# Thirty-two experts on one core: pairs sorted by load, some cut into four parts of 32 rows, gathers issued one scatter earlier

## The chip, the cores and the metric

The kernel runs on 1 core of one Trainium2 chip. Its time is in device microseconds (us), from one execution of the whole program; the median of several executions stands for a kernel. The engines are PE (TensorE, matrix products), DVE (VectorE), ACT (ScalarE), POOL (GpSimd) and SP (SyncE), which here only issues DMAs. "PEld" rows are PE's loads of the stationary operand. TensorE's clock has two levels, 1.2 and 2.4 GHz; the profile shows the granted share (1.00 or 0.50).

## The reference

The program is two transformer blocks over 512 tokens of width 1024. The change lies in the last stage, a mixture of 32 experts with two experts chosen for each token:

```python
hf = h.reshape(-1, d_)                                   # 512 x 1024
g_logits = hf @ w_rg + b_rg                              # 4 groups; the best one is taken
e_sel = take(e_logits.reshape(-1, 4, 8), g_idx)          # its 8 experts; the best two are taken
weights = pg_top * pe_top / sum(pe_top)                  # 512 x 2
for e in range(N_EXPERTS):                               # 32
    act = silu(hf @ w_gate[e]) * (hf @ w_up[e])          # 1024 -> 256
    y = y + combine[:, e:e+1] * (act @ w_down[e])        # 256 -> 1024
```

There are 1024 choices (512 tokens, two each). Counting them with the reference on its inputs gives these loads, for experts 0 to 15: 39, 70, 43, 25, 39, 44, 50, 74, 35, 40, 48, 23, 34, 23, 28, 19, and for experts 16 to 31: 32, 18, 11, 17, 13, 16, 15, 18, 16, 27, 16, 44, 45, 47, 14, 41.

## The kernel before

Everything up to the expert stage is a long run of split matrix products (`pieces`) fed by slabs of weights from SP. It is not changed. The rows of the second normalisation are written to DRAM (`h2_dram`), unsorted, and the residual to the output (`out_columns`).

The expert stage works in **tiles** of 128 rows. Tile `t` carries two experts, 64 rows (`CAP`) for each: one from 0 to 15, one from 16 to 31. An expert with more than 64 rows overflows; its further rows are packed in blocks of 64. Tile 3 (`OVER`) holds the first two such blocks and loads the weights of their experts again. So there are 17 tiles (`BASE`), and behind an `If` (`more_tiles`) up to 13 more with one block each, which are entered where over two blocks are needed. With the loads above two experts (70 and 74 rows) overflow by one block each, so 17 tiles run.

For each tile, in this order:

- POOL `gather(t)`: an indirect DMA brings the tile's rows of `h2_dram` to `Xg`, by the row numbers in `tok` (or `tok2`, which come later). Two buffers.
- PE `transpose_rows(t)` (L3058); ACT and DVE copy the result, scaled, to `XT` (`xt_copy`, L1516, L2452).
- PE `gate_up(t)` (L3080): eight steps over the width, in each one product of 512 columns for each half, its output in PSUM partitions 0 to 63 or 64 to 127, so in one or the other half of the array's columns. A float32 product shows as two records, so a tile has 32.
- ACT `silu`, DVE `gated` (L2457), PE `transpose_act` (L3066), ACT `act_copy`, PE `down(t)` (L3097): 16 records.
- DVE `y_scaled(t)` (L2465) to `Yt`, then POOL `scatter(t)` (L977): an indirect DMA that adds the rows to the output. A scatter waits for the one before it to have landed. The tile `OVER` needs two, one for each half (`tokover`), since a token can stand in both.

PE puts `transpose_rows(t + 1)` between `gate_up(t)` and `transpose_act(t)`. SP loads the weights of expert `e` in three DMAs of 1 MiB, gate and up into one of 7 slots, down into one of 6. A gate/up slot is used again when the tile seven expert places back has finished `gate_up` (`gu_done`), a down slot when the tile three back has finished `down` (`y_done`). The experts of tiles 0 to 2 are fixed, and most of their weights are loaded before the stage. SP loads tile 3 when the overflow experts are known (`overflow_ready`) and the residual is stored (`out_set`), and then the rest in the order of the experts.

The row numbers come from a chain on DVE: ranks within an expert, `tok` (`tokens_ready`), the places of the overflow rows (`rows_with`, `pairs_with`), then for the overflow tile `tok2` (`over_tokens`) and the gate weights by row (`wtab`). Rank within an expert to row of the tile is a match against the constant vector `iota` by a product on PE (L3028, L3035).

Of the kernel before, what the change touches and what calls it, by code (L numbers as in the profile page):

```python
# [25 lines left out]
P = 128  # L26
# [27 lines left out]
BASE = NE // 2 + 1  # L54
NPAIR = BASE + NOV - 2

OVER = 3
# [264 lines left out]
def shared_events():  # L322
# [19 lines left out]
    for chain, events in CHAINS.items():  # L342
        n = 0
        for event, count in events:
# [15 lines left out]
               ("base_ready", 1), ("tokens_ready", 1), ("spots_ready", 1), ("overflow_ready", 1), ("over_tokens", 1),  # L360
               ("choice_weights", 1)],
# [10 lines left out]
def build_program(nc, a, out):  # L372

    ctx = ExitStack()
    with ctx:
# [155 lines left out]
        inpair = [at("inpair0", T0 + 3.75, [2 * NB, 2, NPAIR], BF16), at("inpair1", 129.8125, [2 * NB, 2, NPAIR], BF16)]  # L531
# [4 lines left out]
        steps7 = [at("steps0", T0 + 7, [NE, 7]), at("steps1", 133.3125, [2 * NB, 7])]  # L536
# [12 lines left out]
        tokover = at("tokover", 111.625, [2], U32)  # L549
        notin = at("notin", 111.65625, [2])  # L550
# [273 lines left out]
        def _(sp):  # L824
# [5 lines left out]
            for s in SLABS:  # L830
# [21 lines left out]
                if s["name"] == ("branch2", 1, 0):  # L852
                    sp.wait_ge(*when("dn_summed", C1))
                    load_expert(sp, 0, 0, 0)
                if s["name"] == ("wo2", 2):
                    sp.wait_ge(*when("m2_lo", KC))
                    load_expert(sp, 0, 1, NE // 2)
                if s["name"] == ("wo2", 3):
                    load_expert(sp, 1, 0, NE // 2 + 1)
# [5 lines left out]
            load_down(sp, 2, 1, NE // 2 + 2)  # L865
            slab_consumed(sp, SLAB_OF[("wo2", 1)])
            load_gate(sp, 2, 0, 2, 1)
            slab_consumed(sp, SLAB_OF[("wo2", 2)])
            load_down(sp, 2, 0, 2)
            load_gate(sp, 2, 1, NE // 2 + 2, 0)  # L870
            sp.wait_ge(*when("dense_ready", len(GROUPS)))
            load_gate_up(sp, 1, 1, 1)
            sp.wait_ge(*when("xg_landed0", 16))
            load_down(sp, 1, 1, 1)
            load_gate(sp, 2, 0, 2, 0)
            load_gate(sp, 2, 1, NE // 2 + 2, 1)
            sp.wait_ge(*when("overflow_ready", 1))
            over = [sp.value_load(eover[0:1, x:x + 1], min_val=0, max_val=NE - 1) for x in range(2)]
            sp.wait_ge(*when("out_set", 16 * 3))
            load_pair(sp, OVER, over)  # L880
            for t in range(OVER + 1, BASE):
                x = t - 1
                load_pair(sp, t, (x + NE // 2, x) if x % 2 else (x, x + NE // 2))
            with sp.If(more_tiles(sp)):
                for t in range(BASE, NPAIR):
                    x = t - BASE + 2
# [8 lines left out]
        def _(pool):  # L895
# [57 lines left out]
            def rows_of_pair(t):  # L953
                return (tok if t < BASE and t != OVER else tok2)[:, t:t + 1]

# [2177 lines left out]
```

## Time and profile before

| | us |
|---|---|
| median of 3 executions | 1674.65 (1673.67 to 1675.97) |
| the profiled execution, its own time | 1674.94 |
| its span, first to last instruction | 1673.1 |
| PE busy | 1575.4 (94%) |
| DVE busy | 824.9 (49%) |
| ACT busy | 542.5 (32%) |
| POOL busy | 84.2 (5%) |

The profile is of one execution; 1.8 us of its time lie outside the span. Busy is not the same as bound: an engine may be busy and still wait at the places that set the end, and a DMA queue has no row in this table. The stage that is changed begins at about 1384 us and reaches to the end.

### The profile page before, as it was taken

How to read it: one execution, taken by the hardware profiler on the slowest of the kernel's cores; microseconds unless marked ns; L12 is line 12 of the kernel's file. 1: busy time of each engine (PE TensorE's matmuls, PEld its weight loads, DVE VectorE, ACT ScalarE, POOL GpSimd, SP SyncE). 2: the span in 40 equal slices, each digit the busy share in tenths (PEclk: the TensorE clock that was granted, in tenths of full speed). 3: DMA queues.
4: the chain of work that ended last, by engine and by line, in shares of the span. 5: the costliest groups of instructions: out<-in, count | busy, mean ns of one | idle time of the engine just before them, and what ended most of it. 6: DMA issues, size and time to landing. Idle time of an engine off the chain costs nothing.

```text
span 1673.1 us, 19707 instructions
## 1 busy us (share of the span) xinstructions
PE 1575.4 (94%) x8009; PEld 1185.0 (71%) x8009; DVE 824.9 (49%) x1442; ACT 542.5 (32%) x881; POOL 84.2 (5%) x106
## 2 busy tenths in 40 slices
PE   8999999999999999999999899999999996888876
PEld 6987777777787788888887688787678884333332
DVE  6556334355364776666223874436663736222211
ACT  5334444344433322222113433332354323111110
POOL 5000000000000000000000010000000001121111
PEclk9999999999999999999999899999999997999998
DMA  5335212212333465565323132312213467999995
GB/s 166 114 101 133 71 52 75 63 64 76 76 101 101 151 196 187 190 207 176 101 101 98 51 102 83 94 51 76 69 58 134 158 238 299 399 411 403 404 408 187
DMA packets 147070, 260.41 MB, mean 156 GB/s; under 512 B 16568, under 2 KB 121316, under 8 KB 133664
## 3 DMA queue, kind: packets, MB, share of 16 engines
q1 hardware_dynamic: 138544, 241.41, 41.1%
q0 software_dynamic: 8432, 17.70, 3.7%
q8 instruction: 65, 1.06, 0.3%
q14 instruction: 29, 0.24, 0.0%
HBM read 253.79 MB, written 15.25 MB: 161 GB/s over the span
## 4 chain that ended last, share of the span: by engine, by line
PE 83%; DVE 8%; issue 4%; ACT 2%; DMA 1%; POOL 0%; POOLq 0%; DVEq 0%; ACTq 0%
PE psum L2499 20%; PE psum L2500 20%; PE psum L2501 20%; PE psum L3080 6%; PE psum L3097 4%; PE psum L2810 1%; PE psum L2799 1%; PE psum L2782 1%; DVE cst L2013 1%; DVE WL L1561 1%; PE psum L3058 1%; PE psum L2704 1%; ACT Sb L1115 1%; DMA Xg<-h_rows,tok 1%; PE psum L2566 1%
## 5 line engine op out<-in xcount | busy, mean ns | idle before, releaser
L2499 PE MATMUL psum<-AHs,WH 128*128 128x512 f32 x744 | 306.8, 412 | 7.5 <-DVE WL L1561 4.6
L1561 DVE TENSOR_TENSOR WL<-raw,WH 128x2048 fp32r<-128x2048 f32 (+1 forms) x100 | 226.7, 2267 | 175.5 <-ACT WH L1030 175.0
L2500 PE MATMUL psum<-ALs,WH 128*128 128x512 f32 x744 | 293.6, 395 | 0.0
L2501 PE MATMUL psum<-AHs,WL 128*128 128x512 f32 x744 | 293.4, 394 | 0.0
L1030 ACT ACTIVATE WH<-raw 128x2048 fp32r<-128x2048 f32 (+1 forms) x100 | 189.0, 1890 | 128.8 <-PE psum L2501 99.3
L2499 PEld LDWEIGHTS psum<-AHs,WH 128*128 128x128 f32 x744 | 142.0, 191 | 45.0 <-DVE ALs L1749 5.8
L2499 PE MATMUL psum<-AH,WH 128*128 128x512 f32 (+1 forms) x464 | 169.0, 364 | 0.0
L2500 PEld LDWEIGHTS psum<-ALs,WH 128*128 128x128 f32 x744 | 142.0, 191 | 31.0 <-issue 3.1
L2500 PE MATMUL psum<-AL,WH 128*128 128x512 f32 (+1 forms) x464 | 163.9, 353 | 0.0
L2501 PEld LDWEIGHTS psum<-AHs,WL 128*128 128x128 f32 x744 | 141.8, 191 | 31.0
L2501 PE MATMUL psum<-AH,WL 128*128 128x512 f32 (+1 forms) x464 | 163.1, 352 | 0.0
L3080 PE MATMUL psum<-WE,XT 128*64 128x512 f32 x544 | 123.3, 605 | 10.0 <-issue 9.2
L3080 PEld LDWEIGHTS psum<-WE,XT 128*64 128x64 f32 x544 | 46.7, 140 | 84.1 <-issue 84.1
L2499 PEld LDWEIGHTS psum<-AH,WH 128*128 128x128 f32 x464 | 87.1, 188 | 16.8 <-issue 6.1
L2501 PEld LDWEIGHTS psum<-AH,WL 128*128 128x128 f32 x464 | 87.3, 188 | 12.4
L3097 PE MATMUL psum<-WE,AT 128*64 128x512 f32 x272 | 68.5, 648 | 28.3 <-issue 27.0
L2500 PEld LDWEIGHTS psum<-AL,WH 128*128 128x128 f32 x464 | 87.3, 188 | 10.4
L2013 DVE SCALAR_TENSOR_TENSOR cst<-araw,pcol,cst 128x256 f32<-128x256 f32 x168 | 81.6, 486 | 6.0
L1530 ACT ACTIVATE sA<-psum 128x256 f32<-128x256 f32 x17 | 6.5, 383 | 198.5 <-PE psum L3080 198.5
L2499 PE MATMUL psum<-FH,WH 128*128 128x512 f32 x176 | 68.6, 390 | 0.0
L2500 PE MATMUL psum<-FLo,WH 128*128 128x512 f32 x176 | 68.5, 389 | 0.0
L2501 PE MATMUL psum<-FH,WL 128*128 128x512 f32 x176 | 68.5, 389 | 0.0
(561 smaller groups left out, 2276.6 us busy)
## 6 DMA issues: line engine op xcount, KB each, us to landing
raw<-w_in SPq DMA_DIRECT2D x45, 1024.0 KB, 5.2
WE<-w_gate SPq DMA_DIRECT2D x34, 1024.0 KB, 21.0
WE<-w_up SPq DMA_DIRECT2D x34, 1024.0 KB, 24.6
WE<-w_down SPq DMA_DIRECT2D x34, 1024.0 KB, 19.8
araw<-w_ada SPq DMA_DIRECT2D x24, 1024.0 KB, 5.6
raw<-w_ffn_in SPq DMA_DIRECT2D x22, 1024.0 KB, 7.8
raw<-w_ffn_out SPq DMA_DIRECT2D x11, 1024.0 KB, 4.8
raw<-w_out SPq DMA_DIRECT2D x8, 1024.0 KB, 5.1
```

The costliest lines, as they stand in the source:

```text
L1030: nc.scalar.activation(WH[:, fed[0] % HL, 0:w], raw[:, fed[0] % RAW, 0:w], ACT.Copy).then_inc(S_("hi_ready"), 1)
L1115: nc.scalar.activation(p, p, ACT.Exp, scale=-1.0, bias=peak, accum_out=stat[:, 20 + m % 4:21 + m % 4]).then_inc(S_("mix_exp"), 1)
L1561: V.tensor_tensor(WL[:, n, 0:w], raw[:, n, 0:w], WH[:, fed[0] % HL, 0:w].bitcast(F32), ALU.subtract).then_inc(S_("lo_ready"), 1)
L2013: ins = V.scalar_tensor_tensor(acc, w[:, c, :], col("c_2", c), acc, ALU.mult, ALU.add)
L2499: MM(dst, lh, rh, start=first, stop=False)
L2500: MM(dst, lh, rl, start=False, stop=False)
L2501: return MM(dst, ll, rh, start=False, stop=last)
L2566: ins = MM(bank(2, 1, NB * n + t), src[:, n, P * t:P * t + P], ones[:, 0:1], start=True, stop=True)
L2704: MM(bank(2 + 2 * (n % 2) + m, P * (i + 1)), qkd[half, 0, h, P * i:P * i + P], qkd[half, 1, h, 0:P * (i + 1)], start=True, stop=False)
L2782: made = [MM(bank(2 + m % 3, parts[m]["L"]), parts[m]["q"], parts[m]["k"], start=True, stop=parts[m]["mask"] is None) for m in (n, n + 1)]
L3080: ins = MM(bank(3)[rows], XT[:, t % 2, P * k + CAP * half:P * k + CAP * half + CAP], GU[gate_up_slot(t, half)].rearrange("p (g k n) -> p k ...
L3097: ins = MM(bank(4 + n)[rows], AT[:, t % 2, P * j + CAP * half:P * j + CAP * half + CAP], WE[(2 * t + half) % SLOTS][:, o:o + 512], start=j ...
```

## The change

There are four parts.

1. **No overflow tile.** `BASE` is 16. The experts of tiles 0 to 2 are fixed as before (now 13 to 15 and 29 to 31, `held`). The other 13 of each side are sorted by load on DVE (`sorted_places`): on the side 0 to 15 the fullest comes to tile 3, on the other side to tile 15. SP reads the experts of tiles 3 to 15 from the result (`order`, `order_ready`).
2. **Four parts.** In tiles 3 and 4 the expert of the first side has 96 rows and the other 32; in tiles 14 and 15 it is the other way round (`WIDE`, `parts_of`). PE works on these tiles in four parts of 32 rows, so with four products in a step where there are two. Whatever does not fit goes behind the `If`, which is now entered by any overflow block. With the loads above, tile 3 has 74 and 11 rows, tile 4 has 70 and 13, tile 5 has 50 and 15, tile 14 has 25 and 44, tile 15 has 23 and 45: everything fits.
3. **Order of the DVE chain.** The places (`widths`, `rows_and_pairs`), `token_weights`, `overflow_tokens`, the weights by row and the overflow numbers move behind the first tiles' own work; so `y_scaled(0)` comes after `gated(1)`, and PE does `overflow_spots` and `weights_by_row` after `gate_up(1)`.
4. **Gathers.** `gather(2)` comes before the loop, and in the loop `gather(t + 3)` stands before `scatter(t)`, where `gather(t + 2)` stood. All scatters are single.

The core of the diff:

```diff
-BASE = NE // 2 + 1
-NPAIR = BASE + NOV - 2
-OVER = 3
+BASE = NE // 2
+NPAIR = BASE + NOV
+HELD = 3
+SORTED = NE // 2 - HELD
+WIDE = 2
...
-            return 16 * (t // 2 + 1 + (t >= OVER and t % 2 == OVER % 2))
+            return 16 * (t // 2 + 1)
+        def held(t, half):
+            return NE // 2 * half + SORTED + t
+        def parts_of(t):
+            if t >= BASE:
+                return [(0, CAP, 0)]
+            if HELD <= t < HELD + WIDE:
+                return [(0, 32, 0), (32, 64, 0), (64, 96, 0), (96, 128, 1)]
+            if t >= BASE - WIDE:
+                return [(0, 32, 0), (32, 64, 1), (64, 96, 1), (96, 128, 1)]
+            return [(0, 64, 0), (64, 128, 1)]
...
-            return eng.value_load(eover[0:1, NOV:NOV + 1], min_val=0, max_val=NOV) > 2
+            return eng.value_load(eover[0:1, NOV:NOV + 1], min_val=0, max_val=NOV) > 0
...
-            sp.wait_ge(*when("overflow_ready", 1))
-            over = [sp.value_load(eover[0:1, x:x + 1], min_val=0, max_val=NE - 1) for x in range(2)]
+            sp.wait_ge(*when("order_ready", 1))
             sp.wait_ge(*when("out_set", 16 * 3))
-            load_pair(sp, OVER, over)
-            for t in range(OVER + 1, BASE):
-                x = t - 1
-                load_pair(sp, t, (x + NE // 2, x) if x % 2 else (x, x + NE // 2))
+            for t in range(HELD, BASE):
+                load_pair(sp, t, [sp.value_load(order[0:1, x:x + 1], min_val=0, max_val=NE - 1)
+                                  for x in (t - HELD, SORTED + t - HELD)])
...
+            gather(2)
             pool.wait_ge(*when("over_tokens", 1))
             for t in range(BASE):
-                if t + 2 < BASE:
-                    gather(t + 2)
+                if t + 3 < BASE:
+                    gather(t + 3)
                 scatter(t)
...
             link(V.tensor_copy(cnt, count))
-            full_blocks(over, cnt, thr[:, 0, :], steps7[0])
-            link(V.memset(base_, 1.0))
-            link(V.tensor_tensor_scan(incl, base_, over, 0.0, ALU.mult, ALU.add))
-            link(V.tensor_tensor(base_, incl, over, ALU.subtract))
             dve.wait_ge(*when("base_used", 1))
-            token_of(tok, 5).then_inc(S_("tokens_ready"), 1)
+            token_of(tok[:, 0:HELD], 5, HELD).then_inc(S_("tokens_ready"), 1)
...
+            def sorted_places():
+                key = movable(incl)
+                link(V.scalar_tensor_tensor(incl, cnt, float(NE), K("expert"), ALU.mult, ALU.subtract))
+                link(V.tensor_tensor(versus, key.unsqueeze(2).to_broadcast(sides), key.unsqueeze(3).to_broadcast(sides), ALU.is_ge))
+                link(V.tensor_reduce(movable(wider), versus, AX_X, ALU.add))
...
+                V.tensor_copy(order, named).then_inc(S_("order_ready"), 1)
...
             dve.wait_ge(*when("h2_stored", 16 * NB))
+            sorted_places()
...
             def pairs(t0, t1):
                 xt_copy(t0)
                 if t0 == 0:
-                    overflow_numbers()
-                    overflow_tokens()
-                    token_weights()
+                    widths()
                 for t in range(t0, t1):
                     gated(t)
+                    if t == 1:
+                        overflow_tokens()
+                        weights_by_row()
+                        y_scaled(0)
+                        overflow_numbers()
                     if t + 1 < t1:
                         xt_copy(t + 1)
                     if t == 0:
-                        weights_by_row()
+                        rows_and_pairs()
+                        token_weights()
+                        continue
                     y_scaled(t)
...
                 for k in range(KC):
-                    for half in halves(t):
-                        rows = slice(CAP * half, CAP * half + CAP)
-                        ins = MM(bank(3)[rows], XT[:, t % 2, P * k + CAP * half:P * k + CAP * half + CAP],
+                    for lo, hi, half in parts_of(t):
+                        ins = MM(bank(3)[lo:hi], XT[:, t % 2, P * k + lo:P * k + hi],
                                  GU[gate_up_slot(t, half)].rearrange("p (g k n) -> p k g n", g=2, k=KC)[:, k],
                                  start=k == 0, stop=k == KC - 1)
```

The order of instructions shows three places. On PE, the first steps of `gate_up(3)`, before. Each row is one product; `WE0` and `WE6` are the slots of the two experts, and "64x512" is the output's shape:

```order
L3097 MATMUL psum<-WE5_158,AT_162 64x512
L3080 MATMUL psum<-WE6_159,XT_160 64x512
L3080 MATMUL psum<-WE0_153,XT_160 64x512
...
L3058 MATMUL psum<-cst_49,Xg_164 128x128 x8
L3066 MATMUL psum<-cst_49,sA_161 128x128 x2
L3097 MATMUL psum<-WE0_153,AT_162 64x512
L3097 MATMUL psum<-WE1_154,AT_162 64x512
```

And of the change, the same steps of tile 3 (its line is L3133 now):

```order
L3149 MATMUL psum<-WE5_158,AT_162 64x512
L3133 MATMUL psum<-WE6_159,XT_160 32x512 x3
L3133 MATMUL psum<-WE0_153,XT_160 32x512
...
L3112 MATMUL psum<-cst_49,Xg_164 128x128 x8
L3120 MATMUL psum<-cst_49,sA_161 128x128 x2
L3149 MATMUL psum<-WE0_153,AT_162 32x512 x3
L3149 MATMUL psum<-WE1_154,AT_162 32x512
```

A step has four products of 32 rows in place of two of 64; three of them read the weights of the fuller expert.

On POOL, from the last store of `h2_dram` on, before (L959 is the gather, L977 the scatter, L983 the residual's last columns):

```order
L990 DMA h2_rows<-h2t3_169 128x1024
L959 DMA Xg_164<-h2_rows,tok_197 128x1024 x2
L983 DMA out<-xtm_165 128x4x256
L959 DMA Xg_164<-h2_rows,tok_197 128x1024
L977 DMA out<-Yt_170,tok_197 512x1024
L959 DMA Xg_164<-h2_rows,tok2_203 128x1024
L977 DMA out<-Yt_170,tok_197 512x1024
...
L959 DMA Xg_164<-h2_rows,tok_197 128x1024
L977 DMA out<-Yt_170,tokover_199 512x1024 x2
L959 DMA Xg_164<-h2_rows,tok_197 128x1024
L977 DMA out<-Yt_170,tok_197 512x1024
```

And of the change (L974, L986, L992):

```order
L999 DMA h2_rows<-h2t3_169 128x1024
L974 DMA Xg_164<-h2_rows,tok_200 128x1024 x2
L992 DMA out<-xtm_165 128x4x256
L974 DMA Xg_164<-h2_rows,tok_200 128x1024
L974 DMA Xg_164<-h2_rows,tok2_205 128x1024
L986 DMA out<-Yt_170,tok_200 512x1024
L974 DMA Xg_164<-h2_rows,tok2_205 128x1024
...
L986 DMA out<-Yt_170,tok_200 512x1024
L974 DMA Xg_164<-h2_rows,tok2_205 128x1024
L986 DMA out<-Yt_170,tok2_205 512x1024
L974 DMA Xg_164<-h2_rows,tok2_205 128x1024
```

Three gathers stand before the first scatter that is issued, then one more, and from then on each gather stands one scatter earlier than it did; the double scatter is gone.

On DVE, from the count of rows by expert to the copy of tile 0's transposed rows, before:

```order
L2366 COPY eN_188<-psum 128x32
L2335 TENSOR_TENSOR steps0_185<-eN_188,thr_201 128x224
L2337 TENSOR_REDUCE eN_188<-steps0_185 128x32
L2368 MEMSET eN_188 128x32
L2369 SCALAR_TENSOR_TENSOR eN_188<-eN_188 128x32
L2370 TENSOR_TENSOR eN_188<-eN_188 128x32
L2354 TENSOR_SCALAR spot_204<-psum 128x30
L2355 TENSOR_TENSOR tok_197<-spot_204,psum 128x30
...
L2341 TENSOR_TENSOR inrow1_178<-iota_171,r8_190 128x1024
L2346 TENSOR_TENSOR cst_49<-cst_49,r8_190 128x240
L2348 TENSOR_TENSOR inpair1_180<-cst_49 128x480
L2452 TENSOR_SCALAR XT_160<-psum,small_51 128x128 x4
```

And of the change:

```order
L2363 TENSOR_SCALAR spot_206<-psum 128x3
L2364 TENSOR_TENSOR tok_200<-spot_206,psum 128x3
L2388 SCALAR_TENSOR_TENSOR eN_191<-eN_191,cst_49 128x32
L2389 TENSOR_TENSOR versus_187<-eN_191 128x338
L2390 TENSOR_REDUCE wider_189<-versus_187 128x2x13
L2391 TENSOR_SCALAR places_204<-wider_189 128x13
L2392 TENSOR_SCALAR places_204<-wider_189 128x13
L2394 TENSOR_TENSOR versus_187<-places_204,cst_49 128x338
L2396 TENSOR_TENSOR versus_187<-versus_187,cst_49 128x338
L2398 TENSOR_REDUCE r8_193<-versus_187 128x26
L2399 CAST order_202<-r8_193 128x26
L2501 TENSOR_SCALAR XT_160<-psum,small_51 128x128 x4
```

Five instructions went from ahead of `tok` to a later place, and between `tok` and the copy `XT` stand nine that make `order`; the whole chain for the overflow rows, which stood there, comes after the copy.

## Rows read from the trace of the kernel before

**Rows 1.** The page: the span.

```profile
span 1673.1 us, 19707 instructions
```

**Rows 2.** Windows: length, busy PE, PEld, DVE, ACT, POOL, clock, DMA share, GB/s.

```profile
1396.00:1400.00 4.00, 0.58 (x8) 0.43 (x8) 3.62 (x13) 0.00 (x0) 0.69 (x1) 0.50 0.00 0
...
1404.00:1648.00 244.00, 203.80 (x950) 87.84 (x948) 58.87 (x142) 37.33 (x101) 41.06 (x31) 0.95 1.02 405
...
1648.00:1649.00 1.00, 0.71 (x4) 0.40 (x6) 0.76 (x2) 0.00 (x0) 0.00 (x0) 1.00 0.66 279
```

**Rows 3.** Chain that ended last, its end: start us, us, what.

```profile
1614.46 7.09 PE psum L3080 x32
...
1630.26 1.37 issue
...
1631.63 7.09 PE psum L3080 x32
...
1641.89 5.35 PE psum L3097 x16
...
1647.24 1.05 issue
...
1648.29 7.10 PE psum L3080 x32
...
1657.44 3.67 PE psum L3097 x16
```

**Rows 4.** The same chain, early tiles and the overflow tile's two scatters.

```profile
1422.38 6.87 PE psum L3080 x32
...
1436.07 6.87 PE psum L3080 x32
...
1465.85 7.97 DMA out<-Yt,tokover
```

**Rows 5.** Timeline at 914 us: start us, us, engine, what, idle before.

```profile
914.05 1.92 PE L2904 MATMUL psum<-nsq,wsq 128*32 128x512 f32 x14
```

**Rows 6.** Timeline, the start of the expert stage.

```profile
1396.40 0.58 PE L3028 MATMUL psum<-inpair,inrow 128*128 128x60 bf16 x8 [2.30 <-DVE inrow L2341]
...
1397.97 0.19 DVE L2354 TENSOR_SCALAR spot<-psum 128x30 f32<-128x30 f32 x1
...
1398.20 0.19 DVE L2355 TENSOR_TENSOR tok<-spot,psum 128x30 uint32<-128x30 f32 x1
...
1399.31 1.30 POOL L959 DMA_INDIRECT Xg<-h_rows,tok  x1 [8.66 <-DVE tok L2355]
...
1403.17 1.95 PE L3058 MATMUL psum<-cst,Xg 128*128 128x128 f32 x8 [6.19 <-DMA Xg<-h_rows,tok]
...
1403.41 1.22 DVE L2341 TENSOR_TENSOR inrow<-iota,r 128x1024 bf16<-128x1024 f32 x1
...
1405.68 1.37 DVE L2452 TENSOR_SCALAR XT<-psum,small 128x128 f32<-128x128 f32 x4
...
1406.96 0.65 DVE L2398 TENSOR_TENSOR ovm<-cst,eN 128x480 f32<-128x480 f32 x1
...
1407.20 8.48 PE L3080 MATMUL psum<-WE,XT 128*64 128x512 f32 x32 [0.79 <-DVE XT L2452]
...
1408.73 0.17 DVE L2404 CAST eover<-r 128x15 int32<-128x15 f32 x1
...
1410.47 0.36 SPq L771 DMA_DIRECT2D WE<-w_gate  x1
```

**Rows 7.** DMA from 1400 us: queue packets, MB, share; issues with us to landing.

```profile
q1 hardware_dynamic: 12528, 91.23, 80.0%
...
q0 software_dynamic: 5184, 8.93, 13.3%
...
WE<-w_gate SPq DMA_DIRECT2D x29, 1024.0 KB, 23.3
...
Xg<-h_rows,tok POOLq DMA_INDIRECT x17, 10.6
```

More of the change, by code:

```diff
@@ L953, in rows_of_pair @@
             def rows_of_pair(t):
-                return (tok if t < BASE and t != OVER else tok2)[:, t:t + 1]
+                return (tok if t < HELD else tok2)[:, t:t + 1]
             def gather(t):
@@ L970, in scatter @@
                     pool.wait_ge(*when("out_set", 16 * 3))
-                if t == OVER:
-                    pool.wait_ge(*when("tokover_ready", 1))
-                for half in range(2 if t == OVER else 1):
-                    if half:
-                        pool.wait_ge(*when(f"y_stored{t % 2}", y_stores(t) - 16))
-                    rows = tokover[:, half:half + 1] if t == OVER else rows_of_pair(t)
-                    pool.indirect_dma_start(out=out[0], out_offset=bass.IndirectOffsetOnAxis(ap=rows, axis=0),
-                                            in_=Yt[:, t % 2, :], in_offset=None, bounds_check=S - 1, oob_is_err=False,
-                                            compute_op=ALU.add).then_inc(S_(f"y_stored{t % 2}"), 16)
+                pool.indirect_dma_start(out=out[0], out_offset=bass.IndirectOffsetOnAxis(ap=rows_of_pair(t), axis=0),
+                                        in_=Yt[:, t % 2, :], in_offset=None, bounds_check=S - 1, oob_is_err=False,
+                                        compute_op=ALU.add).then_inc(S_(f"y_stored{t % 2}"), 16)
             def out_columns(c0, c1):
@@ new lines, in widths @@
+            def widths():
+                link(V.tensor_scalar(wider, places[:, 1, :], HELD - 0.5, None, ALU.is_ge))
+                link(V.scalar_tensor_tensor(wider, places[:, 1, :], HELD + WIDE - 0.5, wider, ALU.is_ge, ALU.subtract))
+                link(V.scalar_tensor_tensor(wider, places[:, 1, :], BASE - WIDE - 0.5, wider, ALU.is_ge, ALU.add))
+                for side in range(2):
+                    half = slice(NE // 2 * side, NE // 2 * side + NE // 2)
+                    link(V.tensor_scalar(cap[:, half], wider[:, half], 64.0 * side - 32.0, float(CAP), ALU.mult, ALU.add))
+                link(V.tensor_tensor(cnt, cnt, cap, ALU.subtract))
+                full_blocks(over, cnt, thr[:, 0, :], steps7[0])
+                link(V.memset(base_, 1.0))
+                link(V.tensor_tensor_scan(incl, base_, over, 0.0, ALU.mult, ALU.add))
+                link(V.tensor_tensor(base_, incl, over, ALU.subtract))
+                for n, x in ((2, places[:, 0, :]), (3, places[:, 1, :]), (4, base_), (7, cap)):
+                    chosen(by_tile[n], x.unsqueeze(1).unsqueeze(1), prod[1])
@@ L2408, in overflow_tokens @@
                 dve.wait_ge(*when("spots_used", 1))
[L2409 to L2413 removed]
+                token_of(tok2, 6, NPAIR).then_inc(S_("over_tokens"), 1)
             def token_weights():
```

146 lines of the change are left out of this document (81 added, 65 removed).

## The prediction, made before the change was run

> **What bounds the kernel now.** I read the page first: the span is 1673.1 us [rows 1]. Then the windows of the expert stage: nothing moves between 1396 and 1400 us, then from 1404 to 1648 us the 16 DMA engines are full (share 1.02, 405 GB/s on average), and at 1648 the stream ends [rows 2]. In the same 244 us PE is busy for 203.8, so both look bound. The chain tells them apart. At the end, PE stands idle before each `gate_up`, 1.37 and 1.05 us for the last two, released by nothing that the profile names ("issue"), so by a landed DMA; the starts of the last three are 1614.46, 1631.63 and 1648.29, 17.2 and 16.7 us apart [rows 3]. Early on they are 1422.38 and 1436.07, 13.69 apart, and PE does not wait for weights [rows 4]. So a tile costs PE 13.69 us and the DMA some 16.7; PE lives on what was loaded ahead until it is used up, and the weights set the end. After the last `gate_up` starts, 24.8 us remain (1673.1 less 1648.29): its products, `down`, the last scatter and its landing.
>
> **The change, part by part.**
>
> *The overflow tile.* A pair of experts less is loaded: six DMAs of 1 MiB, 6.29 MB. After the change the last tile is 15, and its weights stand in the stream where those of tile 15 stood. Tile 15 began at 1631.63, tile 16 at 1648.29: **16.7 us less** [rows 3]. The other way to price it is by the queue: 91.23 MB in 80.0% of 273 us is 2.39 us per MB, so 15.1 us for the pair. The tile's gather and two scatters go as well; all 35 indirect DMAs took 13.3% of 273 us, 1.04 each, so three are 3.1 us at most, and near nothing if time goes by rows, since the same 1024 rows are moved in both kernels [rows 7]. That gives 15.1 to 18.2; I take 16.7, since it holds gathers and scatters in the mix in which they come.
> The Trainium skill ("DMA: Bandwidth & Descriptors", section Specifications) gives the fabric a ceiling of 435 GB/s, by which the pair would be 14.5 us; the trace's 405 is under it, as it must be, and decides.
> The wait of the second scatter for the first (7.97 us in the chain) goes too [rows 4]. I count it at nothing: it held PE, and PE had time, as the waits of rows 3 show. Cover for it is the same as for every delay of PE: 18 us, worked out below.
>
> *The start.* `tok` now waits only for the product on PE, which ends at 1396.98 (1396.40 and 0.58), where its first instruction stood at 1397.97 behind the five that are moved: 1.0 earlier, and the two are shorter [rows 6]. The gather (1399.31) follows, and with its landing PE's transposes (1403.17) and SP's next three loads, which wait for it. I take **0.9 us** off the whole stage. `XT` began at 1405.68, since DVE was busy; ahead of it now stands `sorted_places`: five instructions over 338 elements, each about 0.5 (480 elements take 0.65), and four small ones at the pitch of 0.23, together 3.4, so done at about 1401, before the transposes end at 1404.2. So `gate_up(0)` starts not at 1407.20 but about 1405.8 [rows 6]. The bounds of this term are 0, if the loads follow another event, and 1.4.
> SP waited for the overflow numbers, which were written at 1408.9, and issued at 1410.47; the 1.6 us between are two register reads and the move to the address [rows 6]. `order` is there at 1401, so `out_set` decides, and that comes 0.9 earlier than it did. Each of 13 pairs now has two such reads, 1.6 us of SP; a load lands 23.3 us after its issue [rows 7], so SP is that far ahead, and the reads are hidden. Without that cover they would cost 1.6 a pair.
>
> *DVE's long chain.* `widths` stands behind the copy of tile 0: 10 small instructions (0.23 each), two over 224 elements and eight over 256 (0.4 each by the price above), 6.3 us, from 1405.6 to 1412; `gated(0)` is due after 1405.8 and 8.48, at 1414.7, so it is hidden. After the copy of tile 1, which ends near 1416.8, stand 22 small instructions (5.1 us), `rows_with` (1.22), `pairs_with` (1.1), `full_blocks` (0.5) and `token_weights` (ten small, one over 744 elements: 3.3), together 11.2 us [rows 6]. They end near 1428.0, and `gated(1)` is due near 1428.2, when `gate_up(1)` (start 1421.0, 6.87 long) has ended. Cover is nil to thin. Behind it wait `down(1)`, which now waits for `y_scaled(0)`, and on POOL `gather(3)`, which waits for `over_tokens` at about 1429, lands some 11 us later (10.6 after its issue) [rows 7] and is wanted at about 1441.5. If either is late by 2 or 3 us, PE is late by as much. That is paid from PE's lead: at 13.69 a tile from 1421.0 on, `gate_up(15)` could start at 1612.6, and its weights land at 1630.7, so 18 us of lead. The price in the sum is 0. The slots that SP waits for are freed by `gate_up(0)`, `down(0)` and `gate_up(1)`, all 1.4 us earlier than before, so the stream isn't starved.
>
> *Gathers a scatter earlier.* They can only shorten PE's waits, which are not what ends last: 0.
>
> *Four parts.* A tile has 64 and 32 records where it had 32 and 16. If the four columns of the array work side by side, as two do now, a step stays at 0.443 us (7.09 over 16) [rows 3]. The kernel has such products already: at 914 us, 14 records of 32 columns and 512 elements in float32, each round in four column groups, took 1.92 us [rows 5]. Two abreast they would need 7 steps, 3.1 us; four abreast 4 steps, 1.77. So four do run side by side, 0.15 over the ideal, which is the tail of the last record. My price is 0; the upper bound by this row is 8%, so 0.9 us of a tile's 10.8 (7.10 and 3.67). Only tile 15's counts in full: tile 14 starts 17.2 us before its successor, and PE needs 13.69, so it has 3.5 to spend.
> The Trainium skill ("TensorE: Matmul & The Clock Gate", section "Measured speedup vs the span model") lists three column tiles as 2.38 times as fast, not 3; by that the four parts would add a quarter, 2.8 us, and the sum would be 1660. The row at 914 us doesn't show such a loss.
>
> **The sum**, against the profiled execution's own 1674.94 (1673.1 and 1.8 around it): less 16.7, less 0.9, gives 1657.3. That execution lies 0.3 over the median of 1674.65, so I predict **1657.0**.
>
> **Rivals.**
>
> *A: the four parts overlap only partly.* Every row of the array gets four streams of float32 in place of two for 24 steps on end, where the row at 914 us shows under 4. For it speaks that short trial; against it that no step in it is stretched. A tile gets 0.9 to 2.8 us longer, the last one pays: 1658 to 1660, say 1659.5.
>
> *B, the other side: the four parts run two after two.* Then a four-part tile takes 10.8 us more. Tiles 3 and 4 eat 21.5 us, more than PE's lead of 14.6 at tile 14, which starts at 1620.5; tile 15 then follows 24.5 later, at 1645, and the end comes 35.6 behind that: a span of 1680.6, a time of 1682, slower by 7. In general an extra of x above 7.3 us costs 4x less 18, so all of the gain is gone at x = 8.9. Rows 5 speak against it: 1.92 us, not 3.1.
>
> *C: the stream starves at the start.* When PE is at tile 0, SP has but three loads in flight, about 8 us of DMA. If `out_set` or the register reads come late, or `gate_up(0)` does, the DMA stands still, and no one gives that back. Then the 0.9 turns into a loss of 2 to 3: 1660.5. For it speaks that the DMA was at 0 from 1396 to 1400 [rows 2], in the same place; against it that each event moves forward.
>
> *D: the change does not do what it says.* Were there any overflow block, 15 more tiles of 13.69 us would run: some 1860. The counts, 74 and 70 rows in 96, at most 32 in each 32, exclude it unless the kernel counts otherwise.
>
> *E: PE takes over as the bound.* It would need more than 18 us lost before tile 15; only B does that.
>
> **How the numbers follow.** The forecast (the stream shorter by one pair, four parts at no cost, 1655 to 1658.5): 0.73. A: 0.11. C: 0.09. B: 0.04. D: 0.01. Something else, on either side: 0.02. The range takes in A and C above, and below the full 18.2 and 1.4 off, 1655.0, with a little for the tail, which can be shorter or longer by 1.7 us (`down` took 5.35 in one of the last tiles and 3.67 in another) [rows 3]: 1653.8 to 1661.8. A measurement of this kernel can tell 0.2% (3.3 us) from no change; all cases but B, D and some of the rest lie beyond that on the faster side: faster 0.94, the same 0.01, slower 0.05.
>
> **What would show it.** In the profile of the changed kernel: 16 tiles; `gate_up(15)` starting at about 1630.7, with a wait of 1 to 2 us before it; the start of tile 3's `gate_up` 13.7 after that of tile 2; 64 records of 32 columns in about 7.1 us; DMA at 400 GB/s from about 1403 to 1631; the first gather near 1398.4; 24.8 us from the last `gate_up` to the end. I am wrong if a four-part `gate_up` takes much over 7.1 us, if the DMA pauses between 1404 and 1630, or if PE waits for DVE or POOL at the end.

## The result, and the profile after

The changed kernel takes 1663.22 us (median of four executions, 1661.25 to 1666.72), against 1674.81 before: a ratio of 0.9932, 95% interval 0.9918 to 0.9946. It is 11.6 us faster where 17.6 were forecast, and 1.4 us above the range. The direction was right and the size wrong.

The page and the windows of the changed kernel (columns as in [rows 2]):

```profile
span 1664.9 us, 20130 instructions
...
1404.00:1620.00 216.00, 176.62 (x920) 74.26 (x922) 61.70 (x166) 33.01 (x89) 34.98 (x27) 0.95 1.01 401
1620.00:1630.00 10.00, 8.86 (x70) 3.09 (x70) 1.41 (x2) 0.00 (x0) 1.55 (x1) 1.00 0.97 386
1630.00:1640.00 10.00, 7.99 (x54) 3.00 (x46) 1.79 (x5) 2.16 (x6) 0.00 (x0) 0.83 0.54 206
1640.00:1650.00 10.00, 8.17 (x74) 3.05 (x78) 1.83 (x3) 0.77 (x2) 1.55 (x1) 1.00 0.36 93
```

The stream no longer ends at once. Before, the DMA engines were full (1.02) up to 1648, and some 4 us later they were done [rows 2]. Now they are full up to about 1628, and then busy for about half of the time until about 1642: the share is 0.57 from 1630 to 1635 and 0.51 from 1635 to 1640. (The window 1640 to 1650 holds the end of that, and then the rows of a scatter.) The end of the chain shows what this does to PE:

```profile
1507.06 6.87 PE psum L3133 x32
...
1534.95 4.37 issue
1539.32 8.54 PE psum L3133 x32
...
1570.16 3.73 issue
1573.88 10.03 PE psum L3133 x32
...
1624.13 7.07 PE psum L3133 x64
...
1639.71 0.54 issue
1640.25 7.11 PE psum L3133 x64
...
1649.41 3.67 PE psum L3149 x32
```

The first long wait for weights (4.37) comes at tile 9; before, the first over 1 us stood at 1579.71, tile 12 (1.58). The last tile starts at 1640.25, not at 1630.7. What follows it is 24.65 us (1664.9 less 1640.25), as forecast. `gate_up` of tile 11 took 10.03 us in place of 6.87 behind the 3.73 us in which PE stood still; the granted clock of the stretch 1560 to 1600 was 0.91, so part of it ran at 1.2 GHz.

The landings answer to [rows 7] (issues with us to landing, from 1402 us on):

```profile
q1 hardware_dynamic: 11664, 84.94, 76.1%
...
WE<-w_down SPq DMA_DIRECT2D x27, 1024.0 KB, 28.7
WE<-w_gate SPq DMA_DIRECT2D x27, 1024.0 KB, 19.3
WE<-w_up SPq DMA_DIRECT2D x27, 1024.0 KB, 29.4
```

The 6.29 MB are gone (91.23 less 84.94). And SP's own rows show a new wait. They give how long an issue holds SP (ns, min/median/max), from 1440 to 1640 us. Of the kernel before:

```profile
L790 SPq DMA_DIRECT2D WE<-w_down x24: 328/583/8670, 1449.8 to 1625.5; - x24
L771 SPq DMA_DIRECT2D WE<-w_gate x23: 327/438/8284, 1443.0 to 1614.1; - x23
L771 SPq DMA_DIRECT2D WE<-w_up x23: 427/474/4597, 1443.3 to 1616.3; - x23
```

And of the changed one:

```profile
L775 SPq DMA_DIRECT2D WE<-w_gate x22: 332/1229/7874, 1440.5 to 1605.2; - x22
...
L775 SPq DMA_DIRECT2D WE<-w_up x22: 376/2059/3609, 1440.9 to 1612.9; - x22
...
L794 SPq DMA_DIRECT2D WE<-w_down x22: 332/2053/7957, 1452.1 to 1617.3; - x22
```

The median issue took 0.4 to 0.6 us and now takes 1.2 to 2.1. I read this, with the half-empty tail, as some of the 16 engines having more to do than the others. The tail bore that out; for the issue times it explains only a part at best (below).

One caution on start times. What lies ahead of the stage is the same program in the changed kernel and in its variants with the exchange (experiment 2), yet the first gather came at 1400.08 in the one and at 1394.84 in the other. So beside the time I use a **stage length**: from SP's first load that waits for `Xg` to the start of the last tile's `gate_up`. Before, that load was issued here:

```profile
1403.05 0.33 SPq L790 DMA_DIRECT2D WE<-w_down  x1
```

So the length is 245.2 before (1648.29 less 1403.05; 228.6 to tile 15) and 236.3 after (1640.25 less 1403.96). It comes from one profile for each run. Where a kernel was profiled twice, its two lengths lie 0.1, 1.3 and 1.7 us apart, so differences of that size are not read.

### The profile page after: what moved, and what is told of

Its sections match the earlier page's. It is cut to its first block, busy times and chain, and to the rows that moved or that the text cites. A ratio compares the mean times of both kernels' runs of the same rounds, so it can differ in the third digit from the quotient of the medians.

```text
span 1664.9 us, 20130 instructions
## 1 busy us (share of the span) xinstructions
PE 1563.5 (94%) x8143; PEld 1176.8 (71%) x8143; DVE 828.1 (50%) x1458; ACT 540.2 (32%) x875; POOL 79.5 (5%) x103
## 4 chain that ended last, share of the span: by engine, by line
PE 85%; DVE 7%; issue 4%; ACT 2%; DMA 1%; POOL 0%; POOLq 0%; DVEq 0%; ACTq 0%
PE psum L2553 20%; PE psum L2554 20%; PE psum L2555 20%; PE psum L3133 7%; PE psum L3149 4%; PE psum L2864 1%; PE psum L2853 1%; PE psum L2836 1%; PE psum L3112 1%; DVE cst L2023 1%; DVE WL L1571 1%; PE psum L2758 1%; ACT Sb L1125 1%; PE psum L2778 1%; PE psum L2620 1%
## 5 line engine op out<-in xcount | busy, mean ns | idle before, releaser
L3133 PE MATMUL psum<-WE,XT 128*64 128x512 f32 (+1 forms) x640 | 121.4, 621 | 16.7 <-issue 14.8
L3133 PEld LDWEIGHTS psum<-WE,XT 128*64 128x64 f32 (+1 forms) x640 | 42.5, 133 | 93.7 <-issue 93.7
L2554 PEld LDWEIGHTS psum<-AL,WH 128*128 128x128 f32 x464 | 87.9, 190 | 10.3
L3149 PE MATMUL psum<-WE,AT 128*64 128x512 f32 (+1 forms) x320 | 60.1, 619 | 26.6 <-issue 23.2
```

What stands on the lines that cost most here:

```text
L2554: MM(dst, lh, rl, start=False, stop=False)
L3133: ins = MM(bank(3)[lo:hi], XT[:, t % 2, P * k + lo:P * k + hi], GU[gate_up_slot(t, half)].rearrange("p (g k n) -> p k g n", g=2, k=KC)[:, ...
L3149: ins = MM(bank(4 + n)[lo:hi], AT[:, t % 2, P * j + lo:P * j + hi], WE[(2 * t + half) % SLOTS][:, o:o + 512], start=j == 0, stop=j == 1)
```

## The experiments

Before, tiles of an odd expert number had their halves exchanged, so the fuller side, experts 0 to 15 (634 rows against 390), stood in partitions 64 to 127 in every second tile. The change dropped that. It also altered which rows of a half come to which partitions (the line with `low` in experiment 6, where `float(a_)` stood before), which the description of the change leaves out. The counts below use each kernel's own map.
**1. The exchange taken out of the kernel before** (SP's loads follow):

```diff
-                odd = places[:, 0, :].rearrange("p (e j) -> p j e", j=2)[:, 1]
-                link(V.tensor_scalar(odd, odd, -1.0, HOME, ALU.mult, ALU.add))
...
-                load_pair(sp, t, (x + NE // 2, x) if x % 2 else (x, x + NE // 2))
+                load_pair(sp, t, (x, x + NE // 2))
```

> The kernel before, with its swapping of halves in every second tile left out: experts 0 to 15 always stand in rows 0 to 63 of a tile, experts 16 to 31 in rows 64 to 127. The computation is whole. Theory 1 (uneven rows on the DMA engines: a gather or scatter row is moved by the engine that serves its partition, and a tile's weight load lands with its slowest engine): by my count of the rows the fullest engine gets 84 gathered rows in place of 77 (mean 64), and as many scattered ones, so 14 more row moves; at 13.3% of 16 engines over the stage's 273 us for about 2048 row moves, 0.28 us each, that is 4 us: 1678 to 1680 us, with waits for weights that begin earlier than tile 12 and a tail of the stream in which part of the engines is idle. Theory 2 (addresses of the loads read from registers) and theory 3 (gathers issued ahead) expect no change here: 1674.8 us.

Measured: 1679.24, ratio 1.0024 [1.0013, 1.0035], 4.4 us slower than before. The tail appears in the old kernel too:

```profile
1640.00:1650.00 10.00, 8.26 (x44) 3.75 (x40) 1.79 (x5) 2.16 (x6) 0.00 (x0) 1.00 0.67 233
1650.00:1660.00 10.00, 7.57 (x36) 2.65 (x32) 1.67 (x3) 0.39 (x1) 1.55 (x1) 1.00 0.34 106
```

From 1645 to 1650 the share is 0.51. This kernel has no sorting, no early gather, and register addresses for the overflow tile alone, so the tail needs none of them. SP's issues became long here too: medians of 1.98 to 2.11 us, where the kernel before has 0.44 to 0.58.

**2. The exchange put into the changed kernel**, for five of the sorted tiles:

```diff
+SWAPPED = (5, 7, 9, 11, 13)
...
+                if t in SWAPPED:
+                    xs = xs[::-1]
...
+                link(V.tensor_scalar(side, home, -2.0, HOME, ALU.mult, ALU.add))
+                link(V.tensor_tensor(side, side, extra, ALU.mult))
+                link(V.tensor_tensor(side, side, home, ALU.add))
-                link(V.scalar_tensor_tensor(row_, home, CAP / HOME, rk, ALU.mult, ALU.add))
+                link(V.scalar_tensor_tensor(row_, side, CAP / HOME, rk, ALU.mult, ALU.add))
```

(`extra` holds 1 for a row of such a tile. These are eight more operations on DVE, not seven.)

> The changed kernel, with the halves of the sorted tiles 5, 7, 9, 11 and 13 exchanged (the experts of the fuller side stand in rows 64 to 127 there); seven more small operations on DVE before the rows of tile 3 are known. The computation is whole. Theory 1 (uneven rows on the DMA engines): the fullest engine gets 75 gathered rows in place of 89, so 28 fewer row moves at 0.28 us: up to 8 us off, bounded by where the stream's common end stands, so 1655 to 1658 us against 1663.2, the waits for weights begin at tile 12 or later again, and the part of the stage with a DMA share well under 1 becomes shorter than 10 us. Theories 2 and 3 (register addresses, gathers ahead): 1663, no change.

Measured: 1657.55, ratio 0.9895 [0.9878, 0.9912]; the stage is 232.0 long. The stream ends earlier, and its tail is shorter (the share is 0.67 from 1630 to 1635 and 0.04 from 1635 to 1640):

```profile
1620.00:1630.00 10.00, 6.07 (x54) 2.47 (x46) 3.20 (x7) 2.16 (x6) 0.00 (x0) 1.00 0.97 393
1630.00:1640.00 10.00, 7.59 (x69) 2.75 (x70) 0.42 (x1) 0.77 (x2) 1.55 (x1) 1.00 0.35 92
1640.00:1650.00 10.00, 3.62 (x32) 1.08 (x32) 1.41 (x2) 0.00 (x0) 1.54 (x1) 0.80 0.20 27
```

The waits for weights still begin at tile 9 (1.60 us), so that part of the expectation missed.

**3. Addresses as constants** (`KNOWN` holds the order of the experts for this input):

```diff
-                load_pair(sp, t, [sp.value_load(order[0:1, x:x + 1], min_val=0, max_val=NE - 1)
-                                  for x in (t - HELD, SORTED + t - HELD)])
+                load_pair(sp, t, (KNOWN[0][t - HELD], KNOWN[1][t - HELD]))
```

> The changed kernel, with the order of the sorted experts written as constants for this input, so that the weight loads of tiles 3 to 15 have fixed addresses and no register is loaded between them; the rows, the sorting and all waits stay. The result is that of the reference for this input alone. Theory 2 (register addresses delay or scatter the loads): 1657 us and an even end of the stream. Theory 1 (uneven rows on the DMA engines): 1663 us and the same long tail. Theory 3 (gathers ahead): 1663 us.

Measured: 1665.10, ratio 0.9935 [0.9920, 0.9949]. There is no gain: the register reads are hidden, as the prediction had it.

**4 and 5. The gathers' places.** First all of them where they were, then only `gather(2)` early:

```diff
-            gather(2)
             pool.wait_ge(*when("over_tokens", 1))
             for t in range(BASE):
-                if t + 3 < BASE:
-                    gather(t + 3)
+                if t + 2 < BASE:
+                    gather(t + 2)
```

```diff
-                if t + 3 < BASE:
-                    gather(t + 3)
+                if 0 < t < BASE - 2:
+                    gather(t + 2)
```

> The changed kernel, with each gather issued where it stood before: gather of tile t+2 ahead of scatter t, and the first of them behind the wait for the second set of rows. The computation is whole. Theory 3 (the early gathers cost the weight stream something by standing in the DMA queues at a bad time): 1657 us. Theory 1 (uneven rows) and theory 2 (register addresses): the rows moved are the same, so the late landings stay, 1663 us; if the gathers came too late for PE, some us more.

> The changed kernel with only the gather of tile 2 early, ahead of the wait for the second set of rows; from tile 3 on the gathers stand where they stood before (gather of tile t+2 ahead of scatter t). The computation is whole. Theory 5 (the 10.6 us that the gathers' old place cost come from the one gather of tile 2, which then waits behind the late chain of DVE, holds PE for 10 us at tile 1 and with it the slots that SP waits for): 1663 to 1664. Theory 6 (each early gather gives a little, along the whole stage): between 1668 and 1674.

> The changed kernel itself once more, unchanged, beside the two others of this call. Theory 1 and all rivals: 1661 to 1667 us, a median near 1663.5 by the ten runs so far of it and of its twin with constant addresses.

Measured: 1673.81 (ratio 0.9992 [0.9983, 1.0000]) with all in the old place; 1664.74 (0.9930 [0.9916, 0.9943]) with only tile 2's early; 1663.51 (0.9928 [0.9914, 0.9942]) for the changed kernel again. In the first of these the timeline has POOL and PE at tile 2's gather, and the windows what the DMA then does:

```profile
1430.19 1.02 POOL L974 DMA_INDIRECT Xg<-h_rows,tok  x1 [29.03 <-DVE tok L2363]
...
1438.68 1.97 PE L3111 MATMUL psum<-cst,Xg 128*128 128x128 f32 x8 [9.75 <-DMA Xg<-h_rows,tok]
```

```profile
1428.00:1440.00 12.00, 2.25 (x24) 1.94 (x23) 4.45 (x13) 0.38 (x1) 3.67 (x3) 0.73 1.01 397
1440.00:1452.00 12.00, 10.34 (x40) 3.99 (x40) 2.78 (x6) 1.78 (x5) 1.07 (x1) 0.70 0.29 94
```

The first run is 10 us over the 1663 that theories 1 and 2 gave: the gather came too late for PE, and that cost more than "some us". `gather(2)` waits behind the late second table, and PE stands idle for 9.75 us. SP waits 19.0 us for `down` to free a slot and issues its next load at 1448.64 (1438.27 in the changed kernel), and the DMA has little to do for 12 us (share 0.29; 1.02 in the changed kernel), which nothing gives back. So one early gather is worth nearly all of the 10.3 us, and the others nothing that can be told. This is no gain over the kernel before: there `gather(2)` stood behind the same table, but the table came early, and the gather was issued at 1410.21. Part 3 of the change made the table late (the gather is at 1430.19 in this run), and the early gather makes up for it.

**6. The rows in order**, so that few engines carry most of them. The loop over `a_` goes, and two lines take its place:

```diff
-                for a_ in range(8):
-                    low = float(2 * (a_ % 4) + a_ // 4)
...
+                for odd in range(2):
+                    link(V.tensor_scalar(iota[:, 32 * odd:32 * odd + 32], K("expert"), 2.0, float(odd), ALU.mult, ALU.add))
```

> The changed kernel with another map from a row's number to its partition: the even rows of a half stand in order in its first 32 partitions, the odd ones in order in the next 32, in place of the spread by eights. Both halves keep their experts. The computation is whole. Theory 1 (rows on the DMA engines, eight partitions each): by my count the fullest engines get 128 gathered rows in place of 89 (mean 64), and as many scattered ones; 78 more row moves at 0.28 us are 22 us: 1682 to 1688, and the tail of the stream with part of the engines idle becomes some 20 us longer. Theory 1b (only the two halves of the partitions matter, by some port of each half): 1663, no change. Theory 4 (the swap of halves helped through DVE's or SP's timing): 1663, no change.

Measured: 1682.54, ratio 1.0042 [1.0029, 1.0056], 19.0 us over the changed kernel. With only the rows' map changed, even the full part of the stream is slower (381 GB/s, against 401), and PE waits 4 to 5 us ahead of every second tile from tile 7 on, and 1 to 3 ahead of the others:

```profile
1404.00:1620.00 216.00, 166.54 (x868) 68.27 (x866) 57.26 (x151) 28.15 (x78) 33.96 (x26) 0.94 1.00 381
```

In this window the DMA share is 1.00 all the same. So uneven engines do not show as idle ones ahead of the tail, and how the fuller engines slow the stream there is argued, not seen in a row.

**7 and 8. Rows taken away**, from the scatters and from the gathers of tiles 3 to 15:

```diff
-                pool.indirect_dma_start(out=out[0], out_offset=bass.IndirectOffsetOnAxis(ap=rows_of_pair(t), axis=0),
+                pool.indirect_dma_start(out=out[0], out_offset=bass.IndirectOffsetOnAxis(ap=tok2[:, NPAIR - 1:NPAIR], axis=0),
```

```diff
+                rows = tok[:, t:t + 1] if t < HELD else tok2[:, NPAIR - 1:NPAIR]
```

> The changed kernel with all row numbers of the scatters out of bounds, so that each scatter is issued but moves no row: the experts' results are left out of the output. The fullest DMA engine moves 89 rows in place of 178. Theory 1 with one price (0.24 us for a row, gathered or scattered): 21 us less for that engine, and up to 7 us more at the end, where no row of the last scatter is waited for: 1636 to 1642 us (PE's own pace of 13.69 us a tile gives a floor near 1632 to 1639). Theory 7 (only the gathers' rows cost the stream much): 1650 to 1658. Theory 8 (nearly all of the cost lies in the scatters, which read and write each row): the floor, below 1638, and no effect in the run without the gathers' rows.

> The changed kernel with all row numbers of the gathers of tiles 3 to 15 out of bounds: these gathers are issued but bring no row, and the tiles compute with what stands in the buffer. The fullest DMA engine moves 99 rows in place of 178. Theory 1 with one price (0.24 us for a row): 19 us less, 1643 to 1646. Theory 7 (only the gathers' rows cost): the floor, near 1639. Theory 8 (nearly all of the cost lies in the scatters): 1658 to 1663.

Measured: 1643.38 (0.9805 [0.9791, 0.9819]) and 1653.65 (0.9874 [0.9858, 0.9891]). The stage is 217.7 and 225.6 long, so 18.7 and 10.7 shorter. One price for both kinds asked for 1636 to 1642 and 1643 to 1646, and missed both. The theories that put nearly all of the cost on one kind are excluded too. Both kinds of rows cost the stream, a scattered one more. The saving that I expected at the end did not come: from the last `gate_up` (1617.21) to the end of the span (1641.8) it is still 24.6 us.

**9. The choice of tiles that should be most even**, and both choices again side by side. The only edit to the kernel of experiment 2:

```diff
-SWAPPED = (5, 7, 9, 11, 13)
+SWAPPED = (5, 6, 7, 9, 12)
```

> The changed kernel with the halves exchanged in tiles 5, 6, 7, 9 and 12, the choice of five tiles that makes the rows most even by my count for this input: the fullest engine gets 73 gathered rows (75 with tiles 5, 7, 9, 11, 13). The computation is whole. Theory 1 with the price of 0.21 to 0.25 us for a row move that the two runs with other counts gave: 4 row moves less, 1 us off 1657.5, so 1656 to 1657.5; a tail of the stream as short or shorter.

> The changed kernel with the halves of tiles 5, 7, 9, 11 and 13 exchanged, as run before, now beside the evenest choice in one call. Theory 1: 1656.5 to 1658.5 us again. Theory 9 (its four runs fell low by chance, and both choices are the same within what executions differ): 1658 to 1660.

> The changed kernel with the halves of tiles 5, 6, 7, 9 and 12 exchanged, as run before. Theory 1 by the count of all rows alone: at or 1 us under the other kernel of this call. Theory 10 (the count over the whole stage is too coarse: with 5, 6 and 7 exchanged one after the other, and 8, 10, 11 and 13 not, the engines lead and lag in turn, and each tile's landing feels it): 1659.5 to 1661, 2 to 3 us over the other. Theory 9 (chance): the same within 1 us.

Measured: 1660.26 (0.9917 [0.9903, 0.9931]) and 1661.89 (0.9923 [0.9910, 0.9937]) for it; 1659.98 (0.9908 [0.9892, 0.9925]) for the other, so over nine executions a median of 1658.07. The even choice lost twice, by 2 to 3 us. The intervals overlap, but there is no sign of the forecast gain, so the count itself was in doubt. By the count of the next experiments it has 74 rows against 72, so it should lose, but by 1 us only. Whether the order of the exchanged tiles adds to that (theory 10) was not tested apart.

**10 and 11. Which partitions does an engine serve?** I counted again, with an engine that serves four neighbouring partitions and the four that lie 32 further. This is the assignment of the Trainium skill (DMA: Bandwidth & Descriptors, section The descriptor swizzle), stated there for one plain transfer to 128 partitions. Two maps tell the counts apart, both put on top of the exchange of experiment 2. One is the in-order map with the odd rows reversed:

```diff
+                link(V.tensor_scalar(iota[:, 0:32], K("expert"), 2.0, None, ALU.mult))
+                link(V.tensor_scalar(iota[:, 32:64], K("expert"), -2.0, 63.0, ALU.mult, ALU.add))
```

The other keeps the spread by eights and reverses the groups of odd rows:

```diff
-                    low = float(2 * (a_ % 4) + a_ // 4)
+                    low = float(2 * a_ if a_ < 4 else 15 - 2 * a_)
```

> The changed kernel with the halves of tiles 5, 7, 9, 11 and 13 exchanged, and with another map from a row's number to its partition: in each half the even rows stand in order in the first 32 partitions, the odd ones in reverse order in the next 32. The computation is whole. Theory 1a (an engine serves eight neighbouring partitions): the fullest engine gets 128 gathered rows, as in the kernel with the rows in order, which took 1682.5: 1680 or more. Theory 1s (the assignment that the Trainium skill gives in DMA: Bandwidth & Descriptors, section The descriptor swizzle: an engine serves four neighbouring partitions and the four that lie 32 further): the fullest engine gets 72, as with the halves exchanged alone, which took 1658.1 over nine executions: 1657 to 1660.

> The changed kernel with the halves of tiles 5, 7, 9, 11 and 13 exchanged, and with the spread by eights kept, but the order of the four groups of odd rows reversed. The computation is whole. Theory 1a (eight neighbouring partitions): the fullest engine has 75 gathered rows before and after, so no change from 1658.1. Theory 1s (four partitions and the four that lie 32 further): 67 in place of 72; at 0.42 to 0.49 us for a row gathered and scattered, which three earlier differences give when their rows are counted this way, 2.1 to 2.5 us less: 1655.5 to 1656.5, the fastest version so far.

Measured: 1659.97 (0.9898 [0.9881, 0.9915]) and 1656.79 (0.9879 [0.9860, 0.9898]); the kernel before stood at 1676.6 on that chip. The count by eight neighbours fails by 20 us, and the other one holds. An assignment of four neighbours and the four that lie 64 further is excluded as well: by my count it gives 128 rows to the reversed order, as to the order of experiment 6, and 110 or 111 to all kernels with the spread, exchanged or not. No row of a trace names the partitions of an engine; it is these times that bear the assignment out, here for gathers and scatters of rows. The kernel of experiment 6 has no exchange and this one has, so what the reversal is worth by itself was not run; the exchange alone would leave the fullest engine of experiment 6 at 128 rows by either count. The second is the fastest version, 0.3 us above the range expected, though its interval overlaps that of the exchange alone; its last `gate_up` comes 228.9 us behind the first load:

```profile
1404.00:1620.00 216.00, 180.71 (x984) 76.09 (x988) 63.55 (x174) 32.09 (x87) 36.29 (x28) 0.98 1.02 404
1620.00:1630.00 10.00, 5.95 (x54) 2.58 (x50) 3.19 (x7) 2.16 (x6) 0.11 (x1) 0.98 1.00 404
1630.00:1640.00 10.00, 9.00 (x66) 2.54 (x62) 0.42 (x1) 0.39 (x2) 1.45 (x1) 0.85 0.39 111
```

SP's issues are not short again in it, though its engines are the most level:

```profile
L795 SPq DMA_DIRECT2D WE<-w_down x22: 332/1484/6840, 1448.4 to 1606.8; - x22
...
L776 SPq DMA_DIRECT2D WE<-w_up x21: 376/2055/3629, 1442.2 to 1601.8; - x21
```

So uneven rows made the issues long in the kernel before (experiment 1), but even rows do not make them short in the changed one. What else makes them long stays open.

All of them together; "rows" is the number gathered (and again scattered) by the fullest engine, where 64 is the mean:

| kernel | rows, by eight neighbours | rows, by four and four | ratio to before | stage length |
|---|---|---|---|---|
| before (17 tiles) | 77 | 73 | 1 | 245.2 |
| before, sides fixed | 84 | 82 | 1.0024 | 251.7 |
| changed | 89 | 84 | 0.9932, 0.9928 | 236.3, 236.4 |
| changed, rows in order | 128 | 128 | 1.0042 | 254.2 |
| exchange in 5, 7, 9, 11, 13 | 75 | 72 | 0.9895, 0.9908 | 232.0, 230.3 |
| exchange in 5, 6, 7, 9, 12 | 73 | 74 | 0.9917, 0.9923 | 232.5, 231.2 |
| exchange, reversed order | 128 | 72 | 0.9898 | 231.5 |
| exchange, even by fours | 75 | 67 | 0.9879 | 228.9 |

By the third column and the ratios, a row more on the fullest engine, gathered and scattered, costs 0.43 us (18.8 over 44, changed to in order), 0.40 (4.8 over 12, changed to exchange, means of the two ratios) and 0.45 (4.0 over 9, before to fixed sides). The last step, from 72 rows to 67, was worth 1.3 us by the medians and 3.8 by the ratios, too uncertain for a price. The runs without rows give 0.22 for a scattered one (18.7 over 84) and 0.14 for a gathered one (10.7 over 74), together 0.37.

## Why the prediction was right or wrong

**The overflow tile: the step that failed.** "After the change the last tile is 15, and its weights stand in the stream where those of tile 15 stood", so 16.7 us less. The place in the stream was right and the bytes were gone, but the step takes the stream as one pipe, and by the experiments its pace goes with its fullest engine. The stage became 8.9 us shorter, so 7.8 are missing. About 5 of them come back with the exchange (4.8 in time by the ratios, 5.2 in stage length). Its fullest engine has 72 rows, about as many as in the kernel before (73), and there the stage is 13.2 and 14.9 us shorter than before in the two profiles. So the pair is worth 13 to 15 us in this measure, nearer to the 15.1 that the prediction worked out by the queue and set aside. The 16.3 that the last kernel saves (228.9) is not the pair's alone, since its rows are more even (67) than those before. The text priced rows by their number ("near nothing if time goes by rows, since the same 1024 rows are moved in both kernels") and never asked where they land. The dropped exchange stood in the diff (`odd` and SP's order), and no part of the prediction spoke of it. In time, the exchange alone is 17.6 and 15.4 us faster than before by its two ratios, where 17.6 was forecast for the change. So whether the rest of the miss, 0 to 2 us, is real stays open.

**The start: right, but small.** PE's product L3028 stood at 1396.40 [rows 6] and its successor at 1398.32, 1.92 later in this execution; the gather stood at 1399.31 and now at 1400.08, only 0.77 later. So it gained 1.15, where 0.9 was forecast. `gate_up(0)` (1407.87) gained 1.25 of the 1.4, but took 9.41 us in place of 8.48, with a granted clock of 0.50 in the window 1404 to 1410.

**DVE's long chain: right in its effect.** `gate_up(1)` started at 1423.98, not at 1421.0, and PE's lead paid for it, as the prediction said. The four-part tile 3 started 13.78 us behind tile 2, where 13.7 was forecast:

```profile
1438.24 6.87 PE psum L3133 x32
...
1452.02 7.00 PE psum L3133 x64
```

**The gathers: right sum, wrong word.** "They can only shorten PE's waits, which are not what ends last: 0." The prediction took `gather(2)`'s new place for granted in its timing of the chain. Without that place the change would lose 10.3 us, since PE's wait early on holds up the slots and with them the stream. PE's lead of 18 us doesn't cover a wait that stops the DMA, though the prediction wrote that it covers every delay of PE.

**Four parts: right, rival A refuted.** 64 records took 7.00 and 6.87 us in tiles 3 and 4, 7.07 and 7.11 in tiles 14 and 15, where 32 took 6.87 to 7.10. Three of the four `down` took 3.64 to 3.67; that of tile 14 took 5.33 at a granted clock of 0.71 (1635 to 1640), as two-part ones near the end did before (5.35). At the full clock no step is stretched. The loss of 2.8 us that the prediction estimated from the Trainium skill (TensorE: Matmul & The Clock Gate, section "Measured speedup vs the span model") isn't there.

**The other rivals.** B: no, by the same rows. C: no; the DMA share from 1404 to 1620 was 1.01, with 0.91 in the first 6 us (1.00 before). The stream starves (experiment 4) when the early gather is missing. D: 16 tiles ran. E: no; PE waited for weights at every tile from 8 on but tile 12. None of the rivals held the case that came, and the 0.02 for "something else" was too little for a change that redraws which rows stand where.

## What to carry to other kernels

When a kernel streams weights at the DMA's full rate, count the load of each of the 16 engines, not the sum: here the times go with rows moved by the engine of their partition, and each row more on the fullest one, gathered and scattered, cost 0.4 us. A long tail of the stream with a DMA share near a half was the sign of it in the profile; ahead of the tail the share showed nothing. A wait of PE that would cost nothing by itself cost its full length (9.75 us of wait, 10.3 of time) where it held back the freeing of a slot and the DMA ran dry.

## What the runs showed of the hardware

- Gathered and scattered rows slow a stream of weights by the fullest engine's count: 19 us between 84 and 128 rows of 1024, with the same bytes and the same instructions in the stage (experiment 6).
- The times fit an engine that serves four neighbouring partitions and the four that lie 32 further (1659.97 us for 72 rows), and exclude eight neighbouring ones, by which that kernel would have 128 rows like the one that took 1682.54.
- A scatter that moves no row costs the end as much as one that moves them: 24.6 us from the last `gate_up` to the end in both (experiment 7).
- Issues of 1 MiB loads held SP for 0.4 to 0.6 us in one kernel and 1.2 to 2.1 in another (medians); the cause is only known in part.
